# Five changed orders and two memory blocks with places of their own in a two-layer hybrid decoder trunk

## What is computed

```
per layer:
  h = RMSNorm(x); [z | xBC | dt | q | k | v | g] = h @ w_in
  SSD heads:       xBC = silu(causal conv(xBC)); y = chunked scan of x*dt with decays exp(cumsum(dt*A)),
                   + C @ old state per sample sequence; new states are outputs; gate silu(z), grouped norm
  retention heads: rotary q, k; chunkwise retention with fixed decays, old and new states likewise; gate silu(g)
  x = x + concat(ssd, ret) @ w_out
  memory K, V of the prompt = mem @ w_mk, mem @ w_mv          (16 column blocks of 128; outputs too)
  x = x + cross attention over 256 memory rows
  x = x + MoE: group top-1 of 4, then top-2 of 4 SwiGLU experts, 16 experts in all, hidden width 512
final RMSNorm
```

## Time and profile before

| | |
|---|---|
| three runs, us | 1524.92, 1526.49, 1527.15 (median 1526.49) |
| the profiled execution, us | 1530.97 |
| its span in the trace, us | 1528.8 |
| PE busy, us | 1462.2 of 1528.8 (96%), 7430 matmul instructions |
| DVE, ACT, POOL busy | 35%, 17%, 5% |
| moved by DMA | 397.55 MB, mean 260 GB/s |
| mean granted clock of TensorE | 0.989 |
| chain that ended last | PE 87%, DMA 6%, DVE 3%, ACT 1% |

### The profile page before, as it was taken

The page is one execution under the profiler, slowest core; times in us unless marked ns, Lnnn a source line. Parts: engine busy times, 40 slices in busy tenths (PEclk is TensorE's granted clock), DMA queues, the critical chain, the costliest instruction groups (busy, mean ns, idle before and its releaser), DMA issues.

```text
span 1528.8 us, 17999 instructions
## 1 busy us (share of the span) xinstructions
PE 1462.2 (96%) x7430; PEld 911.7 (60%) x7430; DVE 537.6 (35%) x1141; ACT 256.4 (17%) x573; POOL 78.3 (5%) x138
## 2 busy tenths in 40 slices
PE   8999898999999999999899998998999999999997
PEld 5776667667766644444377776685777666344433
DVE  3323755561123331222234156546511334122213
ACT  1002321230012210101100132212210122010102
POOL 1000310000000000000000021100000000000000
PEclk9999999999999999999999999999999999999999
DMA  8334432785349789999933342428843597999994
GB/s 331 110 110 166 156 99 93 317 336 189 136 172 392 315 343 429 425 426 428 388 123 153 111 176 98 149 85 341 329 155 110 220 413 282 391 425 428 427 427 198
DMA packets 36534, 397.55 MB, mean 260 GB/s; under 512 B 6262, under 2 KB 6838, under 8 KB 11616
## 3 DMA queue, kind: packets, MB, share of 16 engines
q1 hardware_dynamic: 26624, 358.95, 58.5%
q0 software_dynamic: 9696, 37.13, 6.3%
q10 hardware_dynamic: 128, 0.26, 0.1%
HBM read 370.21 MB, written 27.37 MB: 260 GB/s over the span
## 4 chain that ended last, share of the span: by engine, by line
PE 87%; DMA 6%; DVE 3%; ACT 1%; DVEq 1%; issue 1%; ACTq 0%; SPq 0%
PE psum L630 38%; PE psum L1219 13%; PE psum L974 9%; PE psum L1239 7%; DMA ring<-stream 5%; PE psum L1266 4%; PE psum L883 1%; DMA rest<-states_out 1%; PE psum L637 1%; PE psum L642 1%; PE psum L1008 1%; PE psum L1053 1%; PE psum L1071 1%; PE psum L1024 1%; DMA work<-acum_flat 1%; PE psum L1195 1%
## 5 line engine op out<-in xcount | busy, mean ns | idle before, releaser
L630 PE MATMUL psum<-rest,ring 128*128 128x320 f32 x1664 | 458.3, 435 | 0.9 <-issue 0.9
L630 PEld LDWEIGHTS psum<-rest,ring 128*128 128x128 f32 x1664 | 315.4, 191 | 135.2 <-issue 8.6
L630 PE MATMUL psum<-store,ring 128*128 128x256 f32 x512 | 120.6, 391 | 3.2 <-DMA ring<-stream 3.2
L630 PEld LDWEIGHTS psum<-store,ring 128*128 128x128 f32 x512 | 97.6, 194 | 24.6 <-issue 7.0
L974 PE MATMUL psum<-work,ring 128*128 128x320 f32 x384 | 104.9, 433 | 0.9 <-ACT work L1401 0.9
L974 PEld LDWEIGHTS psum<-work,ring 128*128 128x128 f32 x384 | 72.3, 190 | 30.9 <-ACT work L1401 1.8
L1219 PE MATMUL psum<-ring,work 128*64 128x512 f32 x384 | 86.1, 594 | 1.0 <-DMA ring<-stream 1.0
L1266 PE MATMUL psum<-work 128*128 128x320 f32 x256 | 77.1, 445 | 3.0 <-issue 3.0
L630 PE MATMUL psum<-work,ring 128*128 128x320 f32 x256 | 72.5, 446 | 7.5 <-DMA ring<-stream 7.5
L1692 DVE TENSOR_TENSOR x<-x,psum 128x320 f32<-128x320 f32 x32 | 15.6, 487 | 178.7 <-PE psum L974 126.6
L2180 DVE TENSOR_TENSOR x<-x,psum 128x320 f32<-128x320 f32 x128 | 59.5, 484 | 50.9 <-PE psum L1266 47.9
(11 more groups left out here) (317 smaller groups left out, 1533.1 us busy)
## 6 DMA issues: line engine op xcount, KB each, us to landing
ring<-stream SPq DMA_DIRECT2D x97, 2048.0 KB, 11.5
work<-stream SPq DMA_DIRECT2D x24, 2048.0 KB, 23.1
states_out<-stream SPq DMA_DIRECT2D x20, 2048.0 KB, 14.4
store<-stream SPq DMA_DIRECT2D x12, 2048.0 KB, 18.6
rest<-stream SPq DMA_DIRECT2D x12, 2048.0 KB, 21.4
st_out<-states_out POOLq DMA_DIRECT2D x12, 1024.0 KB, 11.4
st_out<-work POOLq DMA_DIRECT2D x6, 1024.0 KB, 5.2
ring<-stream SPq DMA_DIRECT2D x4, 1024.0 KB, 13.5
```

Of the source, the lines that this page charges most:

```text
L630: mm = pe.matmul(out, w[:, a:a + P], rhs[:, j, :], start=(j == 0), stop=(j == KD - 1))
```

## The change

1. **Start.** Only the parameters of layer 0 are loaded first; those of layer 1 go after the third block. The first part of the constants moves from behind slab 0 to behind slab 1, with a semaphore of its own, `s_first`.
2. **Turns of x.** Turns 9 to 11 (first half of the channels) wait for four silus only, turns 12 to 14 for eight, and B for all twelve. ACT and DVE copy in the new order.
3. **The move of x_last.** `x_last` lies over the cumulative sums and a pad that is cleared at the start (`rest` grows by 64 columns) instead of over `h`, and POOL issues its four DMAs after the broadcast of step 5. ACT issues none. The four DMAs of B's first group move from step 5 to step 7 on POOL.
4. **First pair of the MoE.** `unpack(1)` and `turn_picked(2)` stand ahead of the wait for the product, not behind its transposes.
5. **The last spread** stands ahead of the load of the flag and the branch.
6. **Memory blocks 8 and 9.** Their weights (slabs 0 and 1 of block 17) go into `alone`, two places in `decays` and `k_tok` that are dead when `s_o` has reached 3. SP issues them ahead of block 16. The other half of block 17 goes into the first half of slot 2 on the `s_mkv` wait, and the wait for `freed[2]` is gone.

Core of the diff:

```diff
@@ SP
-            sp.dma_start(par[:], params.rearrange("l p n -> p l n")).then_inc(s_const, 16)
+            sp.dma_start(par[:, 0, :], params[0]).then_inc(s_const, 16)
...
+                    if q == Q_STATE[2]:
+                        sp.wait_ge(s_o, (L + 1) * 3)
+                        for i in range(2):
+                            sp.dma_start(alone[i], stream[L * QUADS + Q_MEM[2]][:, i * SLAB:(i + 1) * SLAB])\
+                                .then_inc(s_piece[0], 16)
                     if q == Q_MEM[2]:
                         sp.wait_ge(s_mkv, L * 16 + 6)
-                        sp.dma_start(slots[s][:, 0:2 * SLAB], stream[L * QUADS + q][:, 0:2 * SLAB])\
-                            .then_inc(s_piece[0], 16)
-                        sp.wait_ge(freed[s], n)
-                        sp.dma_start(slots[s][:, 2 * SLAB:], stream[L * QUADS + q][:, 2 * SLAB:])\
+                        sp.dma_start(slots[s][:, 0:2 * SLAB], stream[L * QUADS + q][:, 2 * SLAB:])\
                             .then_inc(loaded[s], 16)
...
-                                sp.dma_start(cst[:, 0:FIRST], consts[:, 0:FIRST]).then_inc(s_more, 16)
+                            if i == 1:
+                                sp.dma_start(cst[:, 0:FIRST], consts[:, 0:FIRST]).then_inc(s_first, 16)
...
@@ PE
+                for half in range(2):
+                    pe.wait_ge(s_silu, L * CC + 4 * (half + 1))
+                    for t in range(3):
+                        turn([xbc[:, 4 * half + i, :] for i in range(4)], t)
                 pe.wait_ge(s_silu, (L + 1) * CC)
-                for t in range(3):
-                    for half in range(2):
-                        turn([xbc[:, 4 * half + i, :] for i in range(4)], t)
...
+                    if p == 0:
+                        unpack(1)
+                        turn_picked(2)
+                        pe.wait_ge(s_hid, n_p + 1)
                     first(transposes([(psum[:, 7, 0:P], hidden[:, 0:P])]))
...
+                spread(PAIRS - 1, range(KD))
                 pe.wait_ge(s_spilt, L + 1)
                 with pe.If(pe.value_load(spilt[P - 1:P, L:L + 1], min_val=0, max_val=1) > 0):
-                    spread(PAIRS - 1, range(KD))
@@ ACT
-                        if step == KD - 1:
-                            for i in (13, 14):
-                                act.wait_ge(s_tout[i % 2], turned_by(L, i))
-                            for j in range(4):
-                                own = (4 + j) * DS
-                                act.dma_start(x_last[32 * j:32 * j + DS, :], x_stage[own:own + DS, :])\
-                                    .then_inc(s_moved_last, 16)
@@ POOL
                     if step == 5:
+                        pool.wait_ge(s_tout[0], turned_by(L, TURNS - 1))
+                        pool.wait_ge(s_moved_x, 128 * L + 64)
+                        move(x_last, x_stage, 1, s_moved_x)
+                    if step == 7:
                         pool.wait_ge(s_tout[1], turned_by(L, 17))
                         move(b_of[2], b_stage, 0, s_moved_b)
```

More of the change, by code:

```diff
@@ L215, in build @@
         decays = view(work, 5120, 2, BANK)
+        alone = [work[:, 5120:5120 + SLAB], work[:, 20036:20036 + SLAB]]
         decays_of = [decays, view(store[:, 1, :], 1024, 2, BANK)]
```

54 lines of the change are left out of this document (30 added, 24 removed).

## The result

The changed kernel takes 1511.59 us (median of 4 runs, 1509.58 to 1514.36) against 1526.02 for the kernel before on the same chip. The ratio is 0.9916, 95% interval 0.9897 to 0.9936, which is 12.8 us less, with 9.8 to 15.7 as its bounds (the medians alone differ by 14.4). Two later sets gave 0.9901 (0.9883 to 0.992) and 0.9903 (0.9886 to 0.9921). The prediction said 12.3 us, 1514.2. The sum holds, but several of its terms don't, and they err in both directions. One of the nine executions of the kernel with x_last's move alone took 2198.46 us at a granted clock of 0.652 and is left out of its ratio. The profiled execution lies at 1511.78 us (span 1509.9), at its own median, while the profiled one of before lay 4.5 above its median; the spans therefore differ by 18.9 us, more than the kernels do. So what follows compares stretches, and the medians say what the whole is worth.

The account below looks back on a forecast made before the run. PE was taken as the bound, busy 1462.2 of 1528.8 us. Terms 0.4 + 0.8 + 5.8 + 5.0 + 0 + 0.3 sum to 12.3 us, taking the median from 1526.49 to 1514.2 us; range 1509.5 to 1519.

Parts of the forecast that it names:

- the 0.4 comes through there: Layer 0 turns of x: the head turn's 0.4 us gain shortens PE's 2.21 us wait at the second scan step.
- both links: Scan steps 7 to 8: ACT freed of four DMA issues, and x_last landed early; 2.9 us a layer.
- Memory blocks: Sample states, memory blocks 8 and 9: two slabs moved earlier let block 18 land sooner; 2.5 us a layer, 5.0 in all.
- it can't be more: Block 18's landing in the sample states: 2.46 us sooner at most, unless its own issue at 293.99 moves.
- the MoE ends with the DMA: MoE: the engines run full until the last gate block lands, so the first pair's gain counts as nothing.
- with the same 197 to 199 us: MoE sign: first issue to last gate block stays 197 to 199 us, with more waiting in the last pair.
- Last spread: End of each layer: layer 0 -0.3 to +0.3 us, layer 1 0 to 0.6; 0.3 us in all.
- Rival (a): Sample states and MoE: the fourth state waits for nothing, MoE adds up to 1.6; gain 14.7 to 19.7 us; chance 0.13.
- Both signs: The sum is wrong if the fourth state starts without a wait, or if the MoE gets shorter.
- Rival (b): Memory blocks: the earlier stores use the freed room, so the edit gives little; gain 7 to 9.5 us; chance 0.15.
- Rival (c): Scan: POOL's moved DMAs hold up step 6's broadcast, the 5.8 us gain is lost, 1520 us; chance 0.06.
- Rival (d): PE's clock drops after MoE block waits, 1.69 us each; slower from the eighth, 1527 us with nine; chance 0.02.

Follow-up runs that it names:

- late-load kernel: Changed kernel with SP's load of ring block 12 issued only once the broadcast for the scan's second step has landed: 1507.35 us, repeated 1503.15 us.

## Why the prediction was right, and where it wasn't

**Start: 0.4 predicted, nothing found.** The first matmul came at 7.54 for 7.48. Half of the parameters' bytes went, but slab 0 didn't land sooner in this pair of traces. The first matmul comes at 7.41 to 8.02 us in the six traces without this edit and at 7.17 to 7.81 in the eight with it, so up to 0.2 us may be there and the rest is scatter. The edit wasn't run alone, and what hid the bytes was not tried.

**Turns: 0.8 predicted, nothing that can be measured.** The step that failed is "the 0.4 comes through there". The stretch of the turns is 0.33 and 0.41 us shorter, but in layer 0 the second scan step doesn't wait for DVE's and ACT's chain alone; behind it stands a broadcast of 256 KB that shares the engines with a 2 MB load. The wait of 2.21 us at 191.03 in the earlier trace rows, read as DVE being late, was that transfer: with the load held back the broadcast lands after 3.7 us instead of 6.5, and PE doesn't wait there at all. In layer 1 the wait did get shorter, 2.79 to 2.24 us. The edit alone gave 1.0015.

**Move of x_last: 5.8 predicted; 3.1 and 3.2 us by the traces, 4.9 by the medians (6.1 by the ratio).** From the first row of step 7 to L843's counterpart PE takes 18.06 us in layer 0 (228.59 to 246.65) where it took 21.13 (226.79 to 247.92), 3.1 less, and 3.2 less in layer 1; 2.9 were predicted. (The absolute shift told for L843, 3.3 us, came out as 1.27 in layer 0, since the second scan step had lost what the turns and more had gained.) The mechanism was as told, both links: no DMA issues on ACT, and x_last landed long before use. In the kernel with this edit alone DVE's row starts at 228.15 (told: 228.0), step 8 at 233.55 (233.5), x_last's first reader at 234.72 (234.7) and L843's counterpart at 244.95 (245.0). Some 0.8 us are given back where the blocks of the sample states are late.

**Memory blocks: 5.0 predicted, 10.6 in the traces, 10.8 by the medians.** This is the term that was mis-sized, by half. The stretch from L843 to L946, the last products of the sample states, went from 81.9 us (247.92 to 329.85) to 76.5 (246.65 to 323.10) in layer 0, and from 81.9 to 76.8 in layer 1. In layer 0 it splits so: the waits for blocks fall from 3.75 to 1.65 us, 2.1 us; slow groups become fast, 5.41 to 3.72, 3.35 to 1.90 and the group behind it 1.34 to 1.14 us, 3.3 us; and 0.15 goes the other way; together 5.3 of 5.5. (The first state's group, 3.52 and now 3.00, gives nothing: the group ahead of it went from 1.95 to 2.48.) In layer 1 the waits fall from 4.51 to 1.10 us, 3.4 us, and the slow groups give 1.5, since one drop of the clock is not gone but stands elsewhere: the third state takes 3.35 us behind the wait of 1.10, where it took 1.91. So the waits are worth 5.4 us in two layers, near the 5.0 told, and the clock 4.9, told as nothing. The granted clock of these stretches shows it, before and after (window, its length, busy times of the engines, PEclk, DMA share, GB/s):

```profile
296.41:301.80 5.39, 5.39 (x18) 4.44 (x19) 1.18 (x2) 0.00 (x0) 0.53 (x1) 0.68 1.03 432
309.80:313.10 3.30, 3.28 (x17) 0.47 (x17) 2.29 (x1) 0.00 (x0) 0.00 (x0) 0.55 1.00 422
```

```profile
304.71:306.60 1.89, 1.89 (x20) 0.40 (x20) 1.42 (x1) 0.07 (x1) 0.00 (x0) 1.00 1.13 481
306.60:311.10 4.50, 4.50 (x26) 3.36 (x25) 4.29 (x3) 0.00 (x0) 0.00 (x0) 1.00 0.99 415
```

A granted clock of 0.5 is the lower of TensorE's two levels (1.2 GHz for 2.4); at 0.68 and 0.55 it was there for some two thirds of the first window and nine tenths of the second. After, it stands at 1.00. The prediction did see the 5.41 beside the 3.72, but held that this would be given back at block 18, and it didn't count block 18's own slow group at all. Nor was "it can't be more" for the landing right: block 18 came 3.9 us sooner after its issue, not 2.46, with the issue where it was in the stretch (46.1 us behind L843 both times). That is no accident of two executions: in layer 0 it took 15.5 to 15.8 us in five traces with the old order, 11.8 to 12.5 in eight with the early loads, and 16.4 with the blocks loaded no earlier. The bytes explain 2.46 of it; the other 1.4 are not explained. Still, PE waits 1.65 us ahead of the fourth state in layer 0, inside the 1 to 3 us told; in layer 1 that wait is gone and 1.10 us stand ahead of the third.

How much of this is the edit and how much the execution? Both layers' stretches together take 160.2 to 163.8 us in five traces without the early loads (before, x_last, turns, first pair, spread), and 148.9 to 157.6 in eight with them. The means differ by 10.0 us, so the size holds, but which group is slow does not: it changes from one execution to the next. Nor does each drop need a wait. In the kernel before the clock is down while the first state runs, TensorE working without a gap (the start, end and length of a window, then PEclk, DMA share, GB/s):

```profile
270.00:275.00 5.00, 0.74 0.45 184
```

The row of that state is in the earlier trace rows: 3.52 us with no idle time ahead, where the kernel with the memory blocks alone takes 1.91. The wait of 2.13 us ahead of step 8 was followed by 3.72 us in the kernel before and, with the memory blocks alone, by 5.41. What makes the clock fall in one execution and not in the next stays open; that the clock's share goes with the waits is the likely reading of these rows and isn't shown by an experiment.

The Trainium skill, TensorE: Matmul & The Clock Gate, section "HAM oscillation — how this bites in real kernels", describes a kernel that waits several microseconds for a DMA in each pass of its loop and starts each pass at the lower clock. The waits here are shorter than those, and the traces agree in part: 1.34, 2.41 and 2.60 us were followed by slow groups, but 1.65 here by a fast one, 1.76 in the kernel with x_last's move alone by a group of 3.72 us, and in the MoE none of the waits up to 1.05 us by anything but the full 3.65.

**First pair: 0 predicted, about 0.5 us a layer where no block is waited for.** Alone it gave 1.0003, and in layer 1 of that trace its half microsecond was waited for at the last gate block, exactly as told. The step that failed is "the MoE ends with the DMA": that was so in the profiled execution of before (waits of 0.64 and 1.04 us in layer 0) and not in the four other traces without the edit, which wait for no block. In the changed kernel "with the same 197 to 199 us" failed too: the last gate block is used 196.5 us after the first issue in layer 0 and 196.3 in layer 1 (1479.92, by its weight load, as the 196.8 were read), with no wait over the ordinary 0.3 us, and from layer 0's first gate block to layer 1's first projection it is 2.6 us shorter (222.77 to 220.20), 1.7 of which are the waits for blocks. One MB more brings waits of 1.5 and 2.6 us back. The transfers thus end within a microsecond or two of PE's need, now on this side and now on that (0.42 us of waiting in one execution of the late-load kernel, 0.96 in one of the changed kernel). What shifts their end by that much stays open. The reading "the DMA is the bound" was right to 2 us, but it isn't enough to price half a microsecond.

**Last spread: 0.3 predicted, 0.8 to 0.9.** Layer 0 gave nothing, as told. In layer 1 the bound of 0.6 was too low: 13.49 to 12.70 us with the edit alone, 0.9 in the changed kernel. At the program's end no projection follows that would pay for the load and the branch.

**The sum.** Measured alone, x_last gives 4.9 us and the memory blocks 10.8, together 15.7 by the medians, and the whole change 14.4, 15.0 and 15.0 in its three sets (12.8, 15.1 and 14.8 by the ratios); the other parts alone give 1.0003, 1.0005 and 1.0015, nothing that can be measured. So that the 12.3 came out near was in part luck: the memory term, too small by half, paid for a start and turns that brought nothing and for what x_last's move gives back at the blocks.

Rival (a), more than the sum, had its direction right, and half of its reason: the fourth state still waits in layer 0 (1.6 to 2.2 us in three traces of the changed kernel) and waits little or not at all in layer 1 (0 to 0.6), and what else was missing was the clock. Both signs that the prediction gave for a wrong sum, a fourth state without a wait and a shorter MoE, appeared in part. Rival (b) fell: the earlier stores did not use the room. Rival (c) fell too: from step 5 on only step 9 waits, 0.63 us, for 0.99 before. Rival (d) had a drop's price right at its low end, 1.5 to 1.7 us, and its place wrong: the drops stand in the sample states, at the second scan step and, in both kernels, just ahead of the first pair (0.66 at 525 to 535 us after), none in the pairs. Its sum was wrong besides: 1514.2 plus nine drops of 1.69 us is 1529.4, not 1527. And the 1.56 us of the check are fourteen times the figure that they were held against, not fifteen.

## What to carry to other kernels

A short wait that is followed by a group of matmuls slower than its twin can cost twice: price the edit that removes it with and without the slow group, look at the granted clock of the window behind the wait, and read the same stretch in several executions before you name its cause, since here one program took 74.6 and 81.9 us for it. When a chain ends in a small transfer, look at what large load was issued just ahead of it: here a 2 MB load 1.9 us ahead cost more than the whole reordering of the turns gained, and one wait on the load's queue won it back. Where two limits lie within a microsecond of each other, a trace tells which one ended last in that execution, not which one an edit will meet; adding a known number of bytes does.

## What the runs showed of the hardware

A broadcast of 256 KB took 3.7 us from issue to landing with the engines free, and 6.5 and 7.9 us behind a 2 MB load from another queue that was issued 1.9 us ahead. TensorE's granted clock fell to 0.55 to 0.76 behind some waits of 1.1 to 3.6 us and not behind others of 1.65, 1.76, 2.21 and 2.24, so that a wait cost its own length in one place and 1.5 to 5.0 us more in another (5.0 behind the 2.13 us of the first late-load execution: 2.99 for 1.90, 2.09 for 1.14 and 6.66 for 3.72). It also fell with no wait ahead, in the first sample state of the kernel before (0.74 from 270 to 275 us). The windows of the changed kernel around the second scan step show the idle stretch still at full clock and what follows at 0.75 (columns as above):

```profile
187.50:191.10 3.60, 0.02 (x1) 0.00 (x0) 2.25 (x8) 1.07 (x2) 0.56 (x1) 1.00 0.07 16
191.14:193.00 1.86, 1.86 (x11) 1.38 (x12) 1.03 (x6) 0.00 (x0) 0.00 (x0) 0.75 0.39 112
```
